# The end of a stick-breaking layer: rounding pair outputs as they come, an earlier two-bank filling, and tile 0 closed first

## The reference, cut to what matters

```python
def stick_breaking_attention(q, k, v):
    ...
    for blk in range(s_ // SB_BLOCK):            # 4 blocks of 128 queries
        ...
        z = jnp.einsum('bhqd,bhkd->bhqk', qb, kp).astype(jnp.float32) * scale
        ...
        log_keep = jnp.where(strict, jax.nn.log_sigmoid(-z), 0.0)
        rev = lax.cumsum(log_keep, axis=3, reverse=True)
        ...
        w = jnp.where(strict, jnp.exp(jax.nn.log_sigmoid(z) + after), 0.0)
        outs.append(jnp.einsum('bhqk,bhkd->bhqd', w.astype(vp.dtype), vp))
...
mix = stick_breaking_attention(qc, kc, vc) @ odd_w_out[o]
h = layer_norm(DEEPNORM_ALPHA * h + mix, ln_mix_g[layer], ln_mix_b[layer])
ffn = swiglu(h, ffn_w1[layer], ffn_w3[layer], ffn_w2[layer])
```

## Time and profile before

| what | value |
|---|---|
| median of 3 runs | 1241.78 us (1241.74 to 1243.6) |
| the profiled execution's own time | 1241.92 us |
| its span in the profile | 1240.0 us |
| mean granted TensorE clock | 0.991 |
| TensorE busy | 1198.5 us (97% of the span) |
| DVE, ACT, POOL busy | 414.7, 421.3, 521.5 us |
| DMA queue | 32% of 16 engines' span |

### The profile page before, as it was taken

How to read it: one execution, slowest core, us unless ns; L and a number is a source line. 1 busy time by engine, 2 the same in 40 slices (tenths; PEclk the granted TensorE clock), 3 DMA queues, 4 the chain that set the end, 5 groups by cost and what they waited for, 6 DMA issues and landing times.

```text
span 1240.0 us, 14915 instructions
## 1 busy us (share of the span) xinstructions
PE 1198.5 (97%) x6197; PEld 974.3 (79%) x6197; DVE 414.7 (33%) x658; ACT 421.3 (34%) x577; POOL 521.5 (42%) x270
## 2 busy tenths in 40 slices
PE   7999989999999999999998999999999999999997
PEld 5877757898888888888886677667988888888885
DVE  7568552721111110000804677755411111110007
ACT  6345564232332222122225455523432233222220
POOL 6796513244444444444353122203644444444440
PEclk9999999999999999999999899999999999999998
DMA  8532315153333333233242211202533333333311
GB/s 212 165 79 61 97 68 170 51 164 91 102 93 94 102 103 95 92 102 102 76 130 73 62 52 52 69 1 68 154 102 102 90 98 102 88 100 102 102 51 68
DMA packets 152642, 117.30 MB, mean 95 GB/s; under 512 B 18688, under 2 KB 138536, under 8 KB 152576
## 3 DMA queue, kind: packets, MB, share of 16 engines
q1 hardware_dynamic: 152576, 116.36, 32.0%
HBM read 112.00 MB, written 3.17 MB: 93 GB/s over the span
## 4 chain that ended last, share of the span: by engine, by line
PE 91%; DVE 4%; ACT 2%; issue 1%; DMA 0%; SPq 0%; DVEq 0%; ACTq 0%
PE ps L1431 18%; PE ps L1432 17%; PE ps L1433 17%; PE ps L1453 9%; PE ps L1455 9%; PE ps L1454 9%; PE ps L1857 1%; PE ps L1833 1%; PE ps L1844 1%; PE ps L1460 1%; PE ps L1873 1%; PE ps L1875 1%; DVE stats L1305 1%; PE ps L1874 1%; PE ps L1582 1%
## 5 line engine op out<-in xcount | busy, mean ns | idle before, releaser
L544 POOL TENSOR_TENSOR wlo<-raw,whi 128x1024 fp32r<-128x1024 f32 x190 | 457.5, 2412 | 662.5 <-ACT whi L644 661.7
L1431 PE MATMUL ps<-xhi,whi 128*128 128x512 f32 (+1 forms) x992 | 379.5, 383 | 2.0 <-ACT ov L897 1.1
L1432 PE MATMUL ps<-xlo,whi 128*128 128x512 f32 (+1 forms) x992 | 374.3, 377 | 0.0
L1433 PE MATMUL ps<-xhi,wlo 128*128 128x512 f32 (+1 forms) x992 | 374.1, 377 | 0.0
L644 ACT CAST whi<-raw 128x1024 fp32r<-128x1024 f32 x190 | 201.5, 1065 | 212.7 <-PE ps L1455 188.9
L1431 PEld LDWEIGHTS ps<-xhi,whi 128*128 128x128 f32 x992 | 187.5, 189 | 44.9 <-issue 7.1
L1433 PEld LDWEIGHTS ps<-xhi,wlo 128*128 128x128 f32 x992 | 187.5, 189 | 34.9
L1432 PEld LDWEIGHTS ps<-xlo,whi 128*128 128x128 f32 x992 | 187.7, 189 | 32.4
L979 DVE TENSOR_TENSOR gt<-ps,sg 128x512 f32<-128x512 f32 x44 | 30.4, 692 | 372.6 <-PE ps L1433 372.6
L1453 PE MATMUL ps<-whi,ghi 128*128 128x512 f32 x352 | 137.1, 390 | 0.0
L1455 PE MATMUL ps<-whi,glo 128*128 128x512 f32 x352 | 137.0, 389 | 0.0
(11 more groups left out here) (210 smaller groups left out, 1069.2 us busy)
## 6 DMA issues: line engine op xcount, KB each, us to landing
raw<-in_ffn_w SPq DMA_DIRECT2D x132, 512.0 KB, 3.7
raw<-in_odd_w_in SPq DMA_DIRECT2D x24, 512.0 KB, 3.8
raw<-in_even_w_in SPq DMA_DIRECT2D x16, 512.0 KB, 4.8
h<-in_x SPq DMA_DIRECT2D x8, 512.0 KB, 5.6
raw<-in_even_w_out SPq DMA_DIRECT2D x8, 512.0 KB, 3.7
raw<-in_odd_w_out SPq DMA_DIRECT2D x8, 512.0 KB, 3.6
bias<-rel_scratch SPq DMA_DIRECT2D x8, 256.0 KB, 4.4
out<-h SPq DMA_DIRECT2D x3, 512.0 KB, 2.6
```

The source lines that it names most:

```text
L544: eng.tensor_tensor(lo, raw_of(b), hi, ALU.subtract).then_inc(w_lo, 1)
L1431: eng.matmul(o_, w_hi_, x_hi_, start=start, stop=False)
L1432: eng.matmul(o_, w_hi_, x_lo_, start=False, stop=False)
L1433: return eng.matmul(o_, w_lo_, x_hi_, start=False, stop=stop)
```

## The change

Three things change. First, oatt goes: pair_out copies pair j into sg[:, j % 2], and pairs 0 to 3 are rounded into new tensors ohi and olo (together the size of oatt), at ticks 6, 9, 12 and 15, one pair at a time; pairs 4, 5 and 6 go to xhi and xlo at ticks 20, 21 and 23. pair_out for j >= 2 waits for mix_lower(j - 2), since it reuses its place in sg. Second, the early parts start at tick 20 instead of 21 (two parts in each of ticks 20 to 22, one in each of 23 and 24), and parts 1, 3 and 7 use bank 7. A part waits for the add of the previous part in its own bank; those in bank 7 also for pair_out of the pair before, and stick_out(6) and stick_out(7) wait for the adds. Third, the mixed rows of tile 0 are issued ahead: (0,5), (0,6), (1,5), (0,7), (1,6), (1,7) as (tile, pair) behind stick_out(7), where it was (0,5), (1,5), (0,6), (1,6), (0,7), (1,7).

```diff
-        oatt, o = put("oatt", [P, KT, S], F32, g_region)
+        ohi, o = put("ohi", [P, KT // 2, S], F32R, g_region)
+        olo, o = put("olo", [P, KT // 2, S], F32R, o)
...
-        MIX_AT = {20: range(EARLY_K), 22: (4, 5), 23: (6,)}
-        EARLY_AT = {n: (2 * (n - 21), 2 * (n - 21) + 1) for n in range(21, 25)}
+        MIX_AT = {6: 0, 9: 1, 12: 2, 15: 3, 20: 4, 21: 5, 23: 6}
+        EARLY_AT = {20: (0, 1), 21: (2, 3), 22: (4, 5), 23: (6,), 24: (7,)}
+        EARLY_BANK = (6, 7, 6, 7, 6, 6, 6, 7)
+
+        def bank_added(i):
+            return max([j + 1 for j in range(i) if EARLY_BANK[j] == EARLY_BANK[i]], default=0)
...
             def pair_out(j):
                 act.wait_ge(opv_done, j + 1)
-                eng.copy(oatt[:, j, :], ps[:, 7, :]).then_inc(o_out, 1)
+                if j >= 2:
+                    act.wait_ge(omix, j - 1)
+                eng.copy(sg[:, j % 2, :], ps[:, 7, :]).then_inc(o_out, 1)
 
             def mix_upper(j):
                 act.wait_ge(o_out, j + 1)
-                act.wait_ge(w_used, OOUT)
-                eng.copy(xhi[:, j, :], oatt[:, j, :]).then_inc(omix_hi, 1)
+                if j >= EARLY_K:
+                    act.wait_ge(w_used, OOUT)
+                eng.copy((ohi if j < EARLY_K else xhi)[:, j, :], sg[:, j % 2, :]).then_inc(omix_hi, 1)
...
             def mix_lower(j):
                 dve.wait_ge(omix_hi, j + 1)
-                tt(xlo[:, j, :], oatt[:, j, :], xhi[:, j, :].bitcast(F32), ALU.subtract).then_inc(omix, 1)
+                hi, lo = (ohi, olo) if j < EARLY_K else (xhi, xlo)
+                tt(lo[:, j, :], sg[:, j % 2, :], hi[:, j, :].bitcast(F32), ALU.subtract).then_inc(omix, 1)
...
-                eng.scalar_tensor_tensor(out=h[:, t, c], in0=h[:, t, c], scalar=ALPHA, in1=ps[:, 6, :], op0=ALU.mult,
-                                         op1=ALU.add).then_inc(early_added, 1)
+                eng.scalar_tensor_tensor(out=h[:, t, c], in0=h[:, t, c], scalar=ALPHA, in1=ps[:, EARLY_BANK[i], :],
+                                         op0=ALU.mult, op1=ALU.add).then_inc(early_added, 1)
...
                 if p:
                     pe.wait_ge(o_out, p)
+                if p >= HEAD_PAIRS - 2:
+                    pe.wait_ge(early_added, 4 if p == HEAD_PAIRS - 2 else len(EARLY))
...
             def early_part(i):
                 t, half = EARLY[i]
-                if i:
-                    pe.wait_ge(early_added, i)
-                else:
+                if i == 0:
                     pe.wait_ge(omix, EARLY_K)
                     pe.wait_ge(qk_out, 2 * KT)
+                if bank_added(i):
+                    pe.wait_ge(early_added, bank_added(i))
+                if EARLY_BANK[i] == 7:
+                    pe.wait_ge(o_out, HEAD_PAIRS - 2 if i < 4 else HEAD_PAIRS - 1)
...
-            for k in range(EARLY_K, KT - 1):
+            def mix_wanted(k):
                 pe.wait_ge(omix, k + 1)
                 pe.wait_ge(w_lo, OOUT + k + 1)
-                if k == EARLY_K:
-                    pe.wait_ge(beta_ready, PIECES)
-                for t in range(2):
-                    mixed_rows(t, k)
-                if k == EARLY_K:
-                    stick_out(HEAD_PAIRS - 1)
-            pe.wait_ge(omix, KT)
-            pe.wait_ge(w_lo, OOUT + KT)
+
+            mix_wanted(EARLY_K)
+            pe.wait_ge(beta_ready, PIECES)
             for t in range(2):
-                mixed_rows(t, KT - 1).then_inc(acc_done, 1)
+                mixed_rows(t, EARLY_K)
+            stick_out(HEAD_PAIRS - 1)
+            mix_wanted(EARLY_K + 1)
+            mixed_rows(0, EARLY_K + 1)
+            mix_wanted(EARLY_K + 2)
+            mixed_rows(0, EARLY_K + 2)
+            mixed_rows(1, EARLY_K + 1)
+            mix_wanted(KT - 1)
+            mixed_rows(0, KT - 1).then_inc(acc_done, 1)
+            mixed_rows(1, EARLY_K + 2)
+            mixed_rows(1, KT - 1).then_inc(acc_done, 1)
```

More of the change, by code:

```diff
@@ L947, in _ @@
                     upper_upto(min(OQK + m + WS, OOUT + WS - 1))
-                for j in MIX_AT.get(n, ()):
-                    mix_upper(j)
+                if n in MIX_AT:
+                    mix_upper(MIX_AT[n])
                 if n > 0 and (n - 1) % 3 == 1:
@@ L1408, in _ @@
                     qk_lower(m)
-                for j in MIX_AT.get(n, ()):
-                    mix_lower(j)
+                if n in MIX_AT:
+                    mix_lower(MIX_AT[n])
                 early = EARLY_AT.get(n, ())
-                if early:
-                    early_add(early[0])
+                for i in early[:1]:
+                    early_add(i)
                 if n > 0 and (n - 1) % 3 != 1:
                     weights_out(n - 1)
-                if early:
-                    early_add(early[1])
+                for i in early[1:]:
+                    early_add(i)
             mix_lower(KT - 1)
@@ L1872, in early_part @@
                     c, w = slice(t * P, (t + 1) * P), slice(half * S, (half + 1) * S)
-                    eng.matmul(ps[:, 6, :], xhi[:, k, c], whi[:, b % WS, w], start=k == 0, stop=False)
-                    eng.matmul(ps[:, 6, :], xhi[:, k, c], wlo[:, b % WS, w], start=False, stop=False)
-                    mm = eng.matmul(ps[:, 6, :], xlo[:, k, c], whi[:, b % WS, w], start=False,
+                    eng.matmul(ps[:, EARLY_BANK[i], :], ohi[:, k, c], whi[:, b % WS, w], start=k == 0, stop=False)
+                    eng.matmul(ps[:, EARLY_BANK[i], :], ohi[:, k, c], wlo[:, b % WS, w], start=False, stop=False)
+                    mm = eng.matmul(ps[:, EARLY_BANK[i], :], olo[:, k, c], whi[:, b % WS, w], start=False,
                                     stop=k == EARLY_K - 1)
@@ L1890, in _ @@
                     oqk(*runs[0])
-                if early:
-                    early_part(early[0])
+                for i in early[:1]:
+                    early_part(i)
                 if n >= 4 and n % 3 == 1:
@@ L1898, in _ @@
                     oqk(*runs[1])
-                if early:
-                    early_part(early[1])
+                for i in early[1:]:
+                    early_part(i)
             def mixed_rows(t, k):
                 return token_rows(OOUT + k, k, 0, D, xhi, xlo, t, 2 * t, 2, k == EARLY_K, k == KT - 1)
-            for k in range(EARLY_K, KT - 1):
+            def mix_wanted(k):
                 pe.wait_ge(omix, k + 1)
                 pe.wait_ge(w_lo, OOUT + k + 1)
-                if k == EARLY_K:
-                    pe.wait_ge(beta_ready, PIECES)
-                for t in range(2):
-                    mixed_rows(t, k)
-                if k == EARLY_K:
-                    stick_out(HEAD_PAIRS - 1)
-            pe.wait_ge(omix, KT)
-            pe.wait_ge(w_lo, OOUT + KT)
-            for t in range(2):
-                mixed_rows(t, KT - 1).then_inc(acc_done, 1)
+            mix_wanted(EARLY_K)
+            pe.wait_ge(beta_ready, PIECES)
+            for t in range(2):
+                mixed_rows(t, EARLY_K)
[9 more added lines that the diff above has]
+            mixed_rows(1, KT - 1).then_inc(acc_done, 1)
             pe.wait_ge(early_added, len(EARLY))
```

## The result

| kernel | median us (runs) | lowest to highest | profiled execution, its span |
|---|---|---|---|
| before | 1241.76 (4) | 1240.56 to 1243.6 | 1241.92, 1240.0 |
| changed | 1233.47 (4) | 1231.68 to 1233.89 | 1231.68, 1229.7 |

The ratio is 0.9927, with a 95% interval of 0.9914 to 0.9939: the change makes the kernel faster, by 9.1 us on this ratio (7.6 to 10.7) and by 8.3 us between the medians. The prediction was 7.65 us. The direction and the places are right; the range is not: 1241.78 x 0.9927 is 1232.7 us, 0.2 under the low end of 1232.9. (The changed kernel's own median, 1233.47, lies inside; but the forecast was worked out from 1241.78, and on that base the ratio decides.)

The account below looks back on a forecast made before the run. TensorE, busy 97% of the span, was taken as the bound, so only its waits or lower-clock time could be won. Gains of 7.0 and 0.65 us summed to 7.65, from 1241.92 to 1234.3, median 1234.1; range 1232.9 to 1237.0 us.

Parts of the forecast that it names:

- the seven waits: TensorE waits before piece 19's transposes and early parts 0, 1, 2, 4, 6, 7: together 5.48 us, 6.32 with refill.
- part 6's 0.78 us: TensorE's wait before early part 6, behind early part 5 in the same bank: forecast to stay, 0.90 us with refill.
- the new wait on wlo: Before tile 0's last rows, TensorE would wait some 0.5 us for the last block's lowered weights.
- Part 1: Stick-breaking stage: rounding pairs as they come removes the 2.51 us wait before early part 0 and the clock drop; cost 0.
- part 2: Early parts one tick sooner in two banks: remaining waits before them go, except 0.90 us before early part 6.
- the reason above: At early part 0, the lower clock, 1.57 us, follows the one long wait; waits of 0.78 us were followed by none.
- my last rival: Early parts: the waits don't go, only change their cause to DVE's queue held by early_add(1); 1237 to 1240 us, 3%.
- The cost of the four moved subtractions: Ticks 6, 9, 12, 15: subtractions held under POOL, yet qk_lower ends 0.55 us before scores need it; cost 0, bounds 0 to 2.8.
- The first rival: After ticks 6, 9, 12, 15 the product starts behind POOL's next operation: 2.55 us each, 1244.3, with clock drops 1250.6; 9%.
- Parts 1 and 2 together: Stick-breaking stage's end: 7.89 us in reach less the 0.90 us wait that stays, gain 7.0 us, bounds 5.4 to 7.9.
- Part 3: Tile 0's mixed rows closed first: 1.36 us sooner less 0.7 us wait and refill, gain 0.65 us, bounds 0 and 1.36.
- half a microsecond of scatter between runs: Allowance for whole-run variation in the low end of the range, 1232.9 us, together with no wait at tile 0's close.

Follow-up runs that it names:

- rounding_only: Changed kernel with rounding as pairs come, but early parts at old ticks, all in bank 6, and old mixed-row order: 1240.43 us, ratio 0.9987 to before.
- slip_1: Changed kernel with one extra unread DVE subtraction in front of each of the four moved ones: 1234.59 us, ratio 0.995 to before.
- slip_2: Changed kernel with two extra unread DVE subtractions in front of each of the four moved ones: 1250.97 us, ratio 1.0073 to before.
- both_more: Changed kernel with early part 5 in bank 7 and the last block's weight cast ahead of ACT's wait for the last pair: 1233.2 us, ratio 0.9924 to before.
- after_again: The changed kernel run again unaltered, compared with the kernel before: 1233.42 us, ratio 0.9932.

## Why the prediction was right or wrong

**The bound and the waits: right.** Six of the seven waits went, part 6's 0.78 us stayed, the clock stayed at 1.00, nothing appeared before 800 us, and the new wait on wlo is 0.54 us.

**Part 1, rounding: the sum was right only together with part 2.** The prediction says "The 2.51 us wait goes, and by the reason above the clock drop with it" under the rounding alone. rounding_only shows that by itself it turns into one of 2.02 us behind DVE's scans, with the same drop, and 0.9 us is gained. My schedule of part 2 had DVE's order in it, but I never laid one out for part 1 alone, so I split the gain wrongly: part 1 alone gives 0.91 of the 4.2 us that I put on it. It is the mechanism of my last rival, a wait that changes its cause to DVE's queue, which I weighed for the whole change only. The total didn't suffer, because the change makes both parts, and the schedule for both together had the scans in their place.

**The cost of the four moved subtractions: right to a tenth.** Forecast: the subtraction ends 0.6 us after POOL's operation, product 0.81 us ahead of POOL's next, qk_lower 0.55 ahead of the scores. Trace: 0.55, 0.83 and 0.61. The Trainium skill's rule of the exclusive lock ("SBUF — State Buffer", the section on two separate sides), by which whoever starts first keeps the ports for its whole instruction, is what slip_1 and slip_2 show with numbers: DVE 0.23 us ahead costs DVE nothing and POOL 0.86; DVE 0.07 us behind costs it 2.2.

**The first rival, priced.** It was put at a slip of 0.8 us and 1244.3 to 1250.6. slip_2 measures 1250.97. The place was slightly off (a scan was caught, not the product, so 2.87 us a tick and not 2.55), and the clock dropped after three of the four waits, one of them at 2.9 us and two at 1.6: 6.1 us in all. That this comes so near to four times 1.57, 6.3, is luck.

**Parts 1 and 2 together: 0.43 us undersized.** 7.43 against 7.0. Laid side by side, the two traces show two terms too small. The sum put 0.12 us of refill on every wait. The start-to-start times say 0.07 to 0.13 for four of the waits that went, but about 0.25 for the two behind a group of four transposes: from 810.74 to part 1 it took 0.94 us, in the changed kernel the same step takes 0.35 (809.18 to 809.53), for a bracket of 0.34. That is 0.13 in all. And the groups of eight transposes at 801.73 and 828.23 took 0.99 and 0.94 us to the next start, where the two that now stand ahead of a part take 0.80 (801.61 to 802.41, and again behind 825.79): 0.33 that no bracket showed. Of the 0.43, 0.14 comes back before the rows behind stick_out(7), as the first group of mixed rows now stands directly behind transposes (1.47 us, not 1.36).

**Part 3: 0.56 against 0.65.** The step is the refill after the wait for wlo: wait and refill cost 0.81 us together, and I put 0.7.

**The range: wrong.** The sum for the change, 7.65, is 0.2 us from the measured 7.84, with errors of +0.43, -0.14 and -0.09 in its parts. The mechanism held; what put the result outside is the size of one term, "half a microsecond of scatter between runs", at the low end. The runs showed a scatter of several microseconds in its place. In these runs the kernel before lies between 1239.41 and 1243.95, and one unaltered mark, the start of piece 21's scores, lies between 797.8 and 801.3 in the profiled executions (before 800.25, changed 797.84, 799.96 and 799.43, both_more 801.30). My estimate is that with four runs on either side this alone can move a ratio by 0.001, over 1 us; the later comparisons of the same kernel gave 0.9932 and 0.9942, which are 1233.3 and 1234.6 us on the same basis, both inside the range. The row was there to see: the three runs shown of before already spread over 1.9 us.

No run isolates what makes the front scatter, but the two first traces show where their 2.4 us come from. 0.6 us are there by the first layer's products at 112 us (112.23 before, 111.60 changed). 1.1 us are a clock drop. In the kernel before it falls behind a wait of 2.79 us that ends at 182.18 (granted clock 0.57 over 182 to 186 us), and the next products start 6.60 us after that. In the changed kernel's trace it falls earlier, behind a wait of 1.89 us that ends at 174.97 (0.50 over 176 to 178 us); it is made up in the wait that follows, which is 1.37 us instead of 2.79, and the step that took 6.60 us takes 5.51. The last 0.7 us follow the wait of 4.85 us before the scores of piece 3, which both kernels have: the clock is low until about 691 us in one (0.51 over 684 to 688, 0.64 over 688 to 692) and is back at 1.00 over 688 to 692 in the other, having fallen inside the wait (0.59 over 680 to 684). Why the clock falls at one wait in one execution and at another in the next stays open.

## What to carry to other kernels

When a wait goes, lay out the in-order queue of the engine that answers next, for that edit alone: a batch moved away here only uncovered the add behind DVE's scans, and it took a second PSUM bank or an earlier tick to get TensorE past it. An operation with two SBUF operands on DVE that was moved under such a POOL operation here was held until that was over (2.47 us for 0.62, and a scan of 127 columns 2.57 for 0.39); work out by how much the next one beats POOL's next start, since on the far side of that edge (slip_2) the same kind of move cost 17.6 us, 4.4 a tick. Measure an edit of under 1% between marks inside the trace (here they repeat to 0.02 us), and give the range of whole runs the full spread that the shown runs have.

## What the runs showed of the hardware that was not expected

- Of four TensorE waits of the same length, 2.87 us, in one kernel, three were followed by a lower granted clock (0.83 and twice 0.91 over 20 us) and one by 1.00. The length of a wait doesn't settle whether the clock falls. Waits of 2.02 and 2.51 us were both followed by a drop, and a wait of 1.74 us near 112 us, the same in every kernel, by a granted clock of 0.50 over 114 to 116 us in after_again and by 1.00 in the first traces of before and changed.
- A POOL subtraction of 128x1024 that starts 0.23 us behind a DVE product takes 3.25 us instead of 2.39: the operation begun first runs through at its own length (1.23).
- The distances between marks repeat to 0.02 us from one execution to the next from the scores of piece 21 to the first FFN product, and to 0.08 from there to the end (371.45 to 371.53 us), while the first 665 us vary by 3.1 (first scores at 663.4 to 666.5) and the stretch from the scores of piece 3 to those of piece 6, between the same two instructions in all, by 0.8 (20.67 to 21.43).
